# Expert weight units over the normalised x, a merged sum in a place of its own, and four places for split weights in the late parts

## What is computed

```python
def mixer_block(x, ...):
    xn = rms_norm(x, norm_g)
    proj = xn @ w_in                       # 1024 x 8200: q, k, v of three branches, gates
    ...
    branches = jnp.stack([y_sb, y_mb, y_ml], axis=0)          # each 256 x 512
    y = jnp.einsum("nbsw,nwd->nbsd", branches, w_branch)
    gates = jax.nn.sigmoid(gate_logits.reshape(bsz, s, N_BRANCH, D_MODEL))
    merged = jnp.einsum("bsnd,nbsd->bsd", gates, y)
    return x + merged @ w_out

def hier_moe_block(x, ...):
    xn = rms_norm(x, norm_g)
    ...                                    # router: one of 4 groups, then 2 of its 8 experts
    hid = silu(xn @ w1[e]) * (xn @ w3[e])  # 32 experts, 1024 -> 256, weights 1 MB each
    ...
    return x + sum_e combine[e] * (hid @ w2[e])
```

## Time and profile before

| | |
|---|---|
| median of 3 runs | 1010.28 us (1008.95 to 1012.12) |
| profiled execution, first to last instruction | 1007.1 us |
| TensorE busy | 961.8 us, 96% |
| VectorE, ScalarE busy | 489.5 us (49%), 470.6 us (47%) |
| GpSimd busy | 24.6 us (2%) |
| transfers | 293.36 MB, 291 GB/s over the span |

### The profile page before, as it was taken

One profiled execution on the slowest core, in us unless ns is written; L12 is line 12 of the kernel. 1 busy time (PEld: TensorE's weight loads), 2 busy tenths in 40 slices (PEclk: granted clock), 3 DMA queues, 4 the chain that ended last, 5 costly groups with the idle time before them and its releaser, 6 DMA issues.

```text
span 1007.1 us, 19121 instructions
## 1 busy us (share of the span) xinstructions
PE 961.8 (96%) x7990; PEld 778.6 (77%) x7990; DVE 489.5 (49%) x851; ACT 470.6 (47%) x723; POOL 24.6 (2%) x42
## 2 busy tenths in 40 slices
PE   8999999999999999987899999999999999999687
PEld 8898899999876666643598988999998766666344
DVE  6465875477853222211273669655696622231112
ACT  7465655565544333321265565564754433333111
POOL 1011000000000000000000110000000000000000
PEclk9999999999999999997999999999999999999979
DMA  9634544556889999999975264535779899999995
GB/s 314 236 125 167 174 168 167 210 189 232 340 337 369 421 420 419 420 420 421 394 262 170 84 212 151 188 126 210 251 247 361 329 379 419 421 419 420 421 420 218
DMA packets 85510, 293.36 MB, mean 291 GB/s; under 512 B 17008, under 2 KB 17072, under 8 KB 60848
## 3 DMA queue, kind: packets, MB, share of 16 engines
q1 hardware_dynamic: 85424, 292.12, 76.0%
HBM read 291.05 MB, written 1.05 MB: 290 GB/s over the span
## 4 chain that ended last, share of the span: by engine, by line
PE 78%; DMA 12%; DVE 5%; ACT 3%; issue 1%; POOL 0%; SPq 0%; DVEq 0%; ACTq 0%
PE ps_a L798 10%; PE ps_a L800 9%; PE ps_a L799 9%; PE ps_b L1134 8%; DMA units_over_splits<-in_w_dram 6%; DMA weight_ring<-in_w_dram 5%; PE ps_b L1156 5%; PE ps_a L782 5%; PE ps_b L1214 5%; PE ps_a L784 4%; PE ps_a L783 4%; PE ps_a L1198 4%; PE ps_b L1081 2%; PE ps_b L1014 1%; DVE w_low L1536 1%
## 5 line engine op out<-in xcount | busy, mean ns | idle before, releaser
L1536 DVE TENSOR_TENSOR w_low<-weight_ring,w_high 128x1024 fp32r<-128x1024 f32 x168 | 203.4, 1234 | 92.5 <-ACT w_high L1246 91.8
L1246 ACT ACTIVATE w_high<-weight_ring 128x1024 fp32r<-128x1024 f32 x166 | 173.5, 1057 | 156.8 <-PE ps_a L800 114.8
L798 PE MATMUL ps_a<-xnT_high,w_high 128*128 128x256 f32 x704 | 200.9, 285 | 1.9 <-DVE xnT_low L1542 1.9
L800 PE MATMUL ps_a<-xnT_high,w_low 128*128 128x256 f32 x704 | 199.0, 283 | 0.0
L799 PE MATMUL ps_a<-xnT_low,w_high 128*128 128x256 f32 x704 | 197.9, 281 | 0.0
L798 PEld LDWEIGHTS ps_a<-xnT_high,w_high 128*128 128x128 f32 x704 | 132.7, 188 | 4.5 <-issue 4.5
L799 PEld LDWEIGHTS ps_a<-xnT_low,w_high 128*128 128x128 f32 x704 | 133.3, 189 | 0.5 <-issue 0.5
L800 PEld LDWEIGHTS ps_a<-xnT_high,w_low 128*128 128x128 f32 x704 | 131.8, 187 | 0.0
L1921 DVE TENSOR_TENSOR y_lo<-ps_b,y_hi 128x512 fp32r<-128x512 f32 x64 | 44.3, 692 | 142.7 <-ACT y_hi L1501 140.5
L1462 ACT ACTIVATE h<-ps_b 128x512 f32<-128x512 f32 x64 | 38.2, 597 | 121.8 <-PE ps_b L1134 121.8
L1214 PEld LDWEIGHTS ps_b<-fold,h 128*128 128x128 f32 x512 | 69.1, 200 | 33.3 <-issue 26.8
(11 more groups left out here) (347 smaller groups left out, 1556.8 us busy)
## 6 DMA issues: line engine op xcount, KB each, us to landing
weight_ring<-in_w_in_dram SPq DMA_DIRECT2D x62, 1024.0 KB, 5.2
units_over_splits<-in_w_dram SPq DMA_DIRECT2D x60, 1024.0 KB, 22.4
units_over_attention<-in_w_dram SPq DMA_DIRECT2D x44, 1024.0 KB, 14.7
weight_ring<-in_w_dram SPq DMA_DIRECT2D x40, 1024.0 KB, 19.3
units_over_branches<-in_w_dram SPq DMA_DIRECT2D x30, 1024.0 KB, 18.2
weight_ring<-in_w_branch_dram SPq DMA_DIRECT2D x12, 1024.0 KB, 5.3
unit_over_gates<-in_w_dram SPq DMA_DIRECT2D x10, 1024.0 KB, 18.0
weight_ring<-in_w_out_dram SPq DMA_DIRECT2D x8, 1024.0 KB, 5.9
```

What stands on the lines that cost most here:

```text
L798: mm(dst, wh, xh, start=row == 0 and s % 2 == 0, stop=False, skip_group_check=True)
L800: last = mm(dst, wl, xh, start=False, stop=row == rows - 1, skip_group_check=True)
L1246: A(mix_buf(whi, i), mix_raw(i), ACT.Copy).then_inc(hi_ready, 1)
L1536: v.tensor_tensor(mix_buf(wlo, i), mix_raw(i), mix_buf(whi, i).bitcast(F32), ALU.subtract).then_inc(lo_ready, 1)
```

## The change

Four edits go together:

1. **Where the sum of the branches is split.** `t.merged` takes it in place of `aT`, over the parts of branches 0 and 1. Two expert units (ring 4 and 5) lie over `aT` now (`units_over_xnT`) and one (ring 9) over branch 2's parts (`unit_over_branch`).
2. **Four places for the split weights from part 72 on.** `split_slot` gives place (i - 72) % 4; a split waits for the part that had its place before. Places 4 and 5 are thus free after parts 70 and 71, and ring units 12 and 13 lie over them. The other four units over the split buffers become ring 14 to 17.
3. **SyncE's order.** Ring 4 and 5 are loaded together behind mixer unit 36, after part 63; ring 12 and 13 together after part 71.
4. **The order on two engines.** ScalarE copies a half of the sum ahead of the two splits that stood before it. VectorE does merge(1, 1) ahead of the splits, and fewer splits before the last ones.

```diff
@@ -43,7 +43,8 @@
 PAIRS = NE // 2
 UNIT = 2048
 PART = UNIT // 2
-SPLITS = 6
+SPLITS, LATE_SPLITS = 6, 4
+LATE_FROM = 72
 
 ONCE_UNITS = (4, 9, 3, 21)
 MIX_RING = 4
@@ -62,6 +63,18 @@
 PLACE = {n: i for i, (n, _) in enumerate(BIG)}
 FIRST_BRANCH, FIRST_OUT = len(BIG), len(BIG) + 3
 MIX_UNITS, MIX_PARTS = 2 * len(STREAM), PARTS * len(STREAM)
+
+
+def split_slot(i):
+
+    return i % SPLITS if i < LATE_FROM else (i - LATE_FROM) % LATE_SPLITS
+
+
+def split_before(i):
+
+    return max((j for j in range(i) if split_slot(j) == split_slot(i)), default=None)
+
+
 TOKEN_MAJOR = {"sbv", "mlv", "mbv", "mbq", "mbk", "if"}
 
 
@@ -206,10 +219,13 @@
     gates_at = r.at
     t.gates = r.sb("gates", [P, NC + 3 * NK, SEQ])
     r = two.again()
+    units_xnT = r.sb("units_over_xnT", [P, 2, UNIT])
+    merged_at = r.again()
+    t.merged = [merged_at.sb(f"merged_{n}", [P, NK, SEQ], F32R) for n in ("high", "low")]
     xn_second = [r.sb(f"xn_second_{n}", [P, D], F32R) for n in ("hi", "lo")]
     once_selT = r.again().sb("unit_over_selectT", [P, UNIT])
     t.selT = [r.sb(f"selectT{i}", [P, HALF, SEQ], F32R) for i in range(2)]
-    units_branch = r.sb("units_over_branches", [P, 3, UNIT])
+    unit_branch = r.sb("unit_over_branch", [P, UNIT])
     xn_first = [r.sb("xn_first_hi", [P, D], F32R)]
     once_XT1 = r.again().sb("unit_over_XT1", [P, UNIT])
     XT1 = r.sb("XT1", [P, NK, BATCH * SLOTS])
@@ -227,10 +243,10 @@
 
     one_, split_ = ([b[:, i, :] for i in range(n)] for b, n in ((units_one, 4), (units_split, 6)))
     t.once = [once_y[:, :], once_XT1[:, :], once_selT[:, :], once_x[:, :]]
-    t.ring = [one_[0], one_[2], one_[1], one_[3], units_branch[:, 0, :], units_branch[:, 1, :], t.ring_a[:, 2, :],
-              units_gate[:, :], t.ring_a[:, 3, :], units_branch[:, 2, :], t.ring_a[:, 0, :], t.ring_a[:, 1, :]]
-    t.ring += [split_[i] for i in (0, 3, 1, 4, 2, 5)]
-    t.ring_a_at, t.split_at = [10, 11, 6, 8], 12
+    t.ring = [one_[0], one_[2], one_[1], one_[3], units_xnT[:, 0, :], units_xnT[:, 1, :], t.ring_a[:, 2, :],
+              units_gate[:, :], t.ring_a[:, 3, :], unit_branch[:, :], t.ring_a[:, 0, :], t.ring_a[:, 1, :]]
+    t.ring += [split_[i] for i in (2, 5, 0, 3, 1, 4)]
+    t.ring_a_at, t.split_at = [10, 11, 6, 8], 14
 
 
     three = whole.again()
@@ -564,7 +580,7 @@
         return t.ring_a[:, i // 2 % MIX_RING, i % 2 * PART:(i % 2 + 1) * PART].rearrange("p (k n) -> p k n", k=2)
 
     def mix_buf(w, i):
-        return w[:, i % SPLITS, :].rearrange("p (k n) -> p k n", k=2)
+        return w[:, split_slot(i), :].rearrange("p (k n) -> p k n", k=2)
 
     def place_of(n):
         return ONCE_UNITS.index(n) if n in ONCE_UNITS else ONCE + turn[n] % RING
@@ -601,8 +617,14 @@
 
     def run_sync(sp):
 
+        def after_part(i):
+            sp.wait_ge(part_used, i + 1)
+
+        def last_in_slot(slot):
+            return max(i for i in range(MIX_PARTS) if split_slot(i) == slot)
+
         def after_branch(b):
-            sp.wait_ge(part_used, PARTS * (FIRST_BRANCH + b + 1))
+            after_part(PARTS * (FIRST_BRANCH + b + 1) - 1)
 
         def split_last(u):
 
@@ -617,6 +639,10 @@
             elif u == 35:
                 sp.wait_ge(mb_s, 2)
                 load_unit(sp, ring_units[1])
+            elif u == 36:
+                after_part(PARTS * FIRST_BRANCH - 1)
+                load_unit(sp, ring_units[4])
+                load_unit(sp, ring_units[5])
             elif u == 37:
                 sp.wait_ge(mb_o, 2)
                 sp.wait_ge(d_ready, 1)
@@ -624,11 +650,10 @@
             elif u == 38:
                 sp.wait_ge(ml_s, 1)
                 load_unit(sp, ring_units[3])
-                after_branch(0)
-                load_unit(sp, ring_units[4])
             elif u == MIX_UNITS - 1:
-                after_branch(1)
-                load_unit(sp, ring_units[5])
+                after_part(LATE_FROM - 1)
+                load_unit(sp, ring_units[12])
+                load_unit(sp, ring_units[13])
                 split_last(38)
                 load_unit(sp, ring_units[6])
                 sp.wait_ge(merged, 4)
@@ -645,8 +670,8 @@
                 load_unit(sp, ONCE_UNITS[1])
                 split_last(41)
                 load_unit(sp, ring_units[11])
-                for i in range(12, RING):
-                    sp.wait_ge(part_used, MIX_PARTS - SPLITS + 2 * ((i - 12) // 2 + 1))
+                for i in range(14, RING):
+                    after_part(last_in_slot(2 * ((i - 14) // 2) + 1))
                     if i == RING - 2:
                         load_unit(sp, ONCE_UNITS[2])
                     load_unit(sp, ring_units[i])
@@ -979,7 +1004,7 @@
         pair = take_pair()
         for q in range(PARTS):
             pe.wait_ge(merged_lo, q // 2 + 1)
-            by_token(PARTS * FIRST_OUT + q, pair, aT, q)
+            by_token(PARTS * FIRST_OUT + q, pair, t.merged, q)
 
 
         pair = take_pair()
@@ -988,7 +1013,7 @@
             hi, lo = part(PARTS * (FIRST_OUT + 1) + q)
             for k in range(2):
                 row = 2 * q + k
-                xh, xl = (x[:, row, tt * P:(tt + 1) * P] for x in aT)
+                xh, xl = (x[:, row, tt * P:(tt + 1) * P] for x in t.merged)
                 mm(dst, xh, hi[:, k, cols], start=row == 0, stop=False)
                 mm(dst, xh, lo[:, k, cols], start=False, stop=False)
                 last = mm(dst, xl, hi[:, k, cols], start=False, stop=row == NK - 1)
@@ -1241,8 +1266,8 @@
                     act.wait_ge(t.ahead[u], 16 * (l + 1))
                 else:
                     act.wait_ge(slot_in[u % MIX_RING], 16 * (u // MIX_RING))
-                if i >= SPLITS:
-                    act.wait_ge(part_used, i - SPLITS + 1)
+                if split_before(i) is not None:
+                    act.wait_ge(part_used, split_before(i) + 1)
                 A(mix_buf(whi, i), mix_raw(i), ACT.Copy).then_inc(hi_ready, 1)
 
         def x_high(b):
@@ -1380,10 +1405,10 @@
         split(2); sigmoid(NC + 2 * NK, NC + 3 * NK, "g5")
         nc.scalar.preload_act_table_set(EXP_LN)
         for half in range(2):
+            act.wait_ge(merged, 5 + half)
+            A(t.merged[0][:, 4 * half:4 * half + 4, :], gates[:, NC + 4 * half:NC + 4 * half + 4, :],
+              ACT.Copy).then_inc(merged_hi, 1)
             split(2)
-            act.wait_ge(merged, 5 + half)
-            A(aT[0][:, 4 * half:4 * half + 4, :], gates[:, NC + 4 * half:NC + 4 * half + 4, :],
-              ACT.Copy).then_inc(merged_hi, 1)
         split(8)
 
         def rstd(tt, summed, done):
@@ -1726,13 +1751,13 @@
         v.tensor_tensor(tb[:, :, 0:256], psA[:, :, 0:256], gates[:, 0:NC, :], ALU.mult).then_inc(ml_prod, 1)
         dve.wait_ge(out_hi, 5)
         v.tensor_tensor(brT[1][:, 2], tb[:, :, 0:256], brT[0][:, 2].bitcast(F32), ALU.subtract).then_inc(ml_e, 1)
-        split(2); merge(1, 1)
+        merge(1, 1); split(1)
         for half in range(2):
-            split(1); merge(2, half); split(1)
+            merge(2, half); split(1)
             dve.wait_ge(merged_hi, half + 1)
             o = slice(4 * half, 4 * half + 4)
-            v.tensor_tensor(aT[1][:, o, :], gates[:, NC + 4 * half:NC + 4 * half + 4, :],
-                            aT[0][:, o, :].bitcast(F32), ALU.subtract).then_inc(merged_lo, 1)
+            v.tensor_tensor(t.merged[1][:, o, :], gates[:, NC + 4 * half:NC + 4 * half + 4, :],
+                            t.merged[0][:, o, :].bitcast(F32), ALU.subtract).then_inc(merged_lo, 1)
         split(8)
```

## The result

| | before | after |
|---|---|---|
| median | 1008.81 us (1008.05 to 1012.12, 6 runs) | 1018.61 us (1013.49 to 1020.45, 6 runs) |
| profiled execution, first to last instruction | 1007.1 us | 1016.6 us |
| TensorE busy | 961.8 us | 966.1 us |
| VectorE, ScalarE busy | 489.5, 470.6 us | 489.4, 470.7 us |

The changed kernel is slower: ratio 1.008, 95% interval 1.0066 to 1.0095, so 8.1 us. The medians are 9.8 us apart: four of the changed kernel's six runs lie at 1018.6 to 1020.5 and two at 1013.5 and 1014.5, and what parts them stays open. The two profiled spans differ by 9.5 us. The forecast was 1017.1 us.

What follows compares the result with a forecast made beforehand. TensorE's progress in parts 80 to 83 was taken to start the load stream that ends each layer. Terms of 2.3 and 1.1 us gave 3.4 per layer, 6.8 for two; added to the median 1010.28, 1017.1 us, range 1012 to 1022.

Steps and rivals of the forecast that it cites:

- The bound: End of each layer: set by an expert load stream that starts with TensorE's progress in parts 80 to 83.
- The first term: Before part 76: splits waiting for four places hold up ScalarE's sigmoid and merge(2, 0); 2.3 us late per layer.
- The second term: Before the router's transposes: VectorE's residual addition stands behind the split of part 83; 1.1 us more per layer.
- The terms at nothing: Four earlier unit loads, SyncE's new wait, earlier merge(1, 1) and the ring's new order: each forecast to cost or gain 0.
- The wait behind mixer unit 36: SyncE: mixer unit 37 lands some 3 + 5 us later, covered by 8 us before ScalarE's first copy; cost 0.
- The rival that the stream absorbs the delay: Expert stream, 290 to 322 us: holes of 2.2 us swallow part of the delay, leaving 1.2 us per layer, 1012.7; chance 0.14.
- The rival of the clock: TensorE's idle before part 76 and the transposes lowers its clock, costing 1.5 to 4 us per layer; chance 0.10.
- no idle below 3.6 us in the expert stages led to it: Argument against a clock fall: TensorE's expected idle of 2.3 us is shorter than the idles compared.
- One falsifier: DMA engines at 286 to 290 us: the forecast falls if they are full there.
- the hole: DMA engines nearly idle at 286 to 290 us, share 0.23; loads moved ahead of it gain nothing and make it larger.
- The size between the layers: Both layers: the same 3.4 us delay in each, moving the layer's end one for one, 6.8 us together.
- that sign: Part 81 to the last unit's landing: the forecast falls if this span changes by more than 1 us.

Runs made afterwards that it cites:

- e6: The kernel before with 16 small matmuls on constants put ahead of TensorE's wait for part 76 in each layer; 1016.29 us, ratio 1.0069 to before.
- e1: The changed kernel with ScalarE's sigmoid of the third branch's gates put ahead of the splits of parts 76 and 77; 1011.15 us, ratio 1.0019 to before.
- e2: As e1, and on VectorE the residual addition also put ahead of the split of part 83; 1009.76 us, ratio 1.0002 to before.
- e10: The changed kernel with only VectorE's residual addition put ahead of the split of part 83; 1016.48 us, ratio 1.0073 to before.
- e3: The changed kernel with six places for split weights again and ring units 12 and 13 loaded after part 79; 1008.21 us, ratio 0.999 to before.
- e5: e2 with ring units 4, 5, 12 and 13 loaded where SyncE had them in the kernel before; 1008.94 us, ratio 1.0 to before.
- e7: The changed kernel run once more, unedited; 1017.68 us, ratio 1.0077 to before.
- e9: The kernel before with 11 small matmuls on constants ahead of the output steps of three more expert pairs; 1007.58 us, ratio 0.9986 to before.
- e4: The changed kernel with 16 small matmuls on constants put ahead of part 76, in TensorE's wait; 1015.99 us, ratio 1.0072 to before.

## Why the prediction was right

- **The bound.** TensorE's progress in parts 76 to 83 moves the end of a layer: e6 shows it with no other edit, for both layers together (the last point has where it fails). Right, and the sum stood on it.
- **The first term, 2.3 us a layer.** Each step came as reckoned, less the 0.17 us: ScalarE idle 4.54 us before the split of part 76, the sigmoid at 261.91 (261.7), merge at 263.84 (263.6), high copy at 266.36 (266.15), low at 267.50 (267.3), part 76 at 268.82 (268.6). The term is 268.82 - 0.17 - 266.27 = 2.4. By time it is worth 3.1 a layer (6.2/2, e1). The 0.7 between them would be half of the 1.5 us that the clock costs in layer 1 (below); no run parts that from what the expert stages make of the delay.
- **The second term, 1.1 us.** The split of part 83 at 281.49 (281.3), the addition at 282.63 (282.45), the transposes at 283.91 (283.7), which is 3.4 us late less the 0.17. By time it is worth 0.85 a layer (1.7/2, e2), in the trace 1.0 (e10).
- **The terms at nothing.** e2 and e3 show that the moved units, the sum's new place and the ring's new order are worth nothing; together they stand within 0.2% of the kernel before. The wait behind mixer unit 36 moved unit 37 to 223.29, and ScalarE's first copy out of it (241.02 in the earlier trace rows) stands at 241.20, later by the 0.17 only. One effect had no term: the loads over `ring_a` go out 2.5 to 8 us later, with TensorE on time (e5). It cost nothing either (e2, e3).
- **The rival that the stream absorbs the delay** fell: the first reload moved by 3.69, and the holes up to 322, which are real slack (5.2 us, e5), swallowed nothing. They are slack for the transfers and not for TensorE, whose delay makes the reloads' places free later.
- **The rival of the clock** had 0.10 and came true in part, in layer 1. The step that failed is "no idle below 3.6 us in the expert stages led to it". It was an observation on some five idles and says nothing on one of 2.2. What it costs: from the low half of the sum to the addition it is 15.13 us in layer 0 (267.50 to 282.63) and 16.67 us in layer 1 (770.58 to 787.25), so 1.5 us. e7 has the same (15.12 and 16.68). Its price stood at 1.5 to 4, at the right low end. The Trainium skill (TensorE: Matmul & The Clock Gate, "HAM oscillation — how this bites in real kernels") describes a TensorE that waits and whose next burst starts at the lower clock. The four falls in six behind the wait of 2.2 us agree with that; the other two waits, and the one of 3.75 us that no fall followed, don't.
- **The number was nearer than the sum.** 1017.1 stood on a median of 1010.28 before, from three runs; over six it is 1008.81. Of the change itself 6.8 us was forecast and 8.1 measured, 9.8 by the medians. 6.8 with the clock's 1.5 is 8.3. That 1017.1 lies so near 1018.61 is partly luck: a base 1.5 us too high made up for a change that was too small.
- **One falsifier was wrong.** I wrote that the forecast falls if the DMA engines are full at 286 to 290. They are, and it holds:

```profile
286.00:290.00 4.00, 4.00 (x30) 3.67 (x28) 1.53 (x3) 2.58 (x6) 0.00 (x0) 1.00 1.01 424
290.00:294.00 4.00, 4.00 (x36) 4.00 (x36) 1.98 (x2) 1.32 (x2) 0.00 (x0) 1.00 0.51 150
```

  Transfers that are through at 286 before end after 290 now. The last load over `ring_a` goes out 8.3 us later (282.75 for 274.49): 2.5 of it come with the new order of the splits (277.00 in e3), 3.0 with the four places (279.99 in e2), and 2.8 with TensorE. I had written that earlier loads make the hole larger; with TensorE on time the share there is 1.01 in e3 and 0.91 in e2, and nothing is lost. So the hole was less proof than I took it for: in e5 there is none, and the early units are still worth nothing.
- **The size between the layers.** I took 3.4 for both, and the end of a layer as moving one for one. Layer 0's mixer gave 3.7, its expert stage 2.05 more; layer 1's mixer 5.05, its expert stage -1.5. I had written that the forecast falls if the span from part 81 to the last landing changes by more than 1 us, and by that sign it falls as well: from the loads behind part 81 (288.81 before, 292.45 now) to the last output step (498.01 and 503.71) layer 0 takes 2.1 us longer and layer 1 1.5 us less (786.29 and 797.08, 996.46 and 1005.79). So one for one holds for the sum of both layers in e6 (6.4 us put in, 7.0 out) and not within a layer. e6 has +1.5 and +0.1 in those stages, with no edit in them. The stretches at half clock lie elsewhere in each trace: in layer 0 the last begins at 456 before, at 476 in the changed kernel and at 475 in e6. That a stretch nearer the end costs more would fit both, but e9 speaks against the clock as the whole cause: with no such stretch in layer 0, that expert stage takes 197.03 us from first reload to last sum (305.85 to 502.88), against 196.63 before (layer 1: 196.24 against 197.96). What moves the expert stages by 1 to 2 us stays open.

## What to carry over

Look at instruction order before the number of buffers: taking places away costs where the instruction that now waits for a place has something urgent queued behind it on its own engine. Here going from six places to four cost 8 us, and two changes of order that put the urgent instruction first gave it all back with four. Loading four units earlier was worth nothing here, since the stream behind them starts when TensorE releases the places. Whether the DMA engines looked busy or idle ahead of that didn't tell: their share at 286 to 290 is 0.23, 0.91 and 1.01 in kernels that take the same time (before, e2, e3).

## What the chip showed that I had not expected

- After 2.2 us without a matmul the granted clock fell from full (2.4 GHz) to half (1.2 GHz) for 3.4 us (a mean of 0.72 over 6 us), in four of six cases (three traces of two layers), and it stayed full in the other two with the same 2.21 us and the same work before. With small matmuls in the wait (e4, e6) it stayed full in all four cases.
- In the expert stage, matmuls on constants in waits that are there anyway raise the mean clock from about 0.984 to 0.999 and the time falls by only 1.4 us (e9, interval 0.1 to 2.7): a low clock was cheap where a transfer sets the end.
- With TensorE on time, the loads that wait for splits went out up to 8 us later (the first at 264.43 for 256.90 in e2, 264.42 in e3), the share of the DMA engines from 254 to 278 fell from 0.88 to 0.67 (e2), and the time stayed the same (1.0002 and 0.999).
